# Overflow branch ahead of the experts, joint norm between two transformer blocks: one change to a float32 kernel on Trainium2

## What is computed

```python
def rms_norm(x, gain):                       # NORM_EPS = 1e-5
    xf = x.astype(jnp.float32)
    y = xf * lax.rsqrt(jnp.mean(xf * xf, axis=-1, keepdims=True) + NORM_EPS)
    return (y * gain.astype(jnp.float32)).astype(x.dtype)

# end of the first block
    for e in range(N_EXPERTS):
        out = out + combine[:, e:e + 1] * swiglu(t, w_gate[e], w_up[e], w_down[e])
    ...
    return rms_norm(h, final_norm)

# second block
    h = jnp.concatenate([meta, x], axis=1)
    for l in range(DEPTH):
        hn = rmsnorm(h, norm_gain[l])        # RMS_EPS = 1e-6
        proj = hn @ w_in[l]
    ...
        h = h + jnp.concatenate([do, fo], axis=-1) @ w_out[l]
    out = rmsnorm(h, final_gain)
    return out[:, N_META:N_META + seq]
```

## Time and profile before

| | us |
|---|---|
| median of 3 executions | 1854.92 |
| lowest, highest | 1848.85, 1860.95 |
| the profiled execution | 1859.74 |
| its span, first to last instruction | 1857.9 |
| TensorE busy | 1705.1 (92%) |
| VectorE busy | 1224.3 (66%) |
| ScalarE busy | 1029.4 (55%) |
| mean granted TensorE clock | 0.930 |

### The profile page before, as it was taken

The page is one execution under the profiler, slowest core; times in us unless marked ns, Lnnn a source line. Parts: engine busy times, 40 slices in busy tenths (PEclk is TensorE's granted clock), DMA queues, the critical chain, the costliest instruction groups (busy, mean ns, idle before and its releaser), DMA issues. The chain is left out here.

```text
span 1857.9 us, 21753 instructions
## 1 busy us (share of the span) xinstructions
PE 1705.1 (92%) x8749; PEld 1420.8 (76%) x8749; DVE 1224.3 (66%) x1305; ACT 1029.4 (55%) x1238; POOL 58.2 (3%) x54
## 2 busy tenths in 40 slices
PE   6988999887799999999999999999598999797997
PEld 5867888787678888888888888888397786587775
DVE  3645554468468888888888888888544544444553
ACT  4735443346367777777767677777544433444352
POOL 0000000013000000000000000000011000020000
PEclk9998999997789999999999999999799977798968
DMA  6323555550259999999999999999754222164200
GB/s 232 136 91 113 181 181 181 181 196 1 96 202 362 364 340 324 333 394 319 349 312 396 321 356 335 356 362 348 207 116 100 84 66 46 46 137 114 68 1 34
DMA packets 133081, 389.31 MB, mean 210 GB/s; under 512 B 8694, under 2 KB 14266, under 8 KB 132844
## 3 DMA queue, kind: packets, MB, share of 16 engines
q1 hardware_dynamic: 132692, 387.14, 61.7%
q10 hardware_dynamic: 280, 0.69, 0.1%
HBM read 386.76 MB, written 1.05 MB: 209 GB/s over the span
## 5 line engine op out<-in xcount | busy, mean ns | idle before, releaser
L192 DVE TENSOR_TENSOR wlo<-raw,whi 128x2048 fp32r<-128x2048 f32 (+1 forms) x286 | 629.1, 2208 | 304.4 <-ACT whi L182 303.0
L182 ACT ACTIVATE whi<-raw 128x2048 fp32r<-128x2048 f32 (+1 forms) x286 | 526.4, 1846 | 267.9 <-PE psum L359 267.9
L357 PE MATMUL psum<-whi,xh 128*128 128x512 f32 (+1 forms) x1280 | 499.8, 390 | 14.9 <-issue 8.6
L359 PE MATMUL psum<-whi,xl 128*128 128x512 f32 (+1 forms) x1280 | 488.6, 382 | 0.0
L358 PE MATMUL psum<-wlo,xh 128*128 128x512 f32 (+1 forms) x1280 | 488.1, 381 | 0.0
L357 PEld LDWEIGHTS psum<-whi,xh 128*128 128x128 f32 x1280 | 244.3, 191 | 72.1 <-DVE wlo L192 11.2
L359 PEld LDWEIGHTS psum<-whi,xl 128*128 128x128 f32 x1280 | 243.9, 191 | 50.3
L358 PEld LDWEIGHTS psum<-wlo,xh 128*128 128x128 f32 x1280 | 244.4, 191 | 46.7 <-issue 0.2
L192 DVE TENSOR_TENSOR wlo<-raw_more,whi 128x2048 fp32r<-128x2048 f32 (+1 forms) x94 | 204.0, 2177 | 39.5 <-ACT whi L182 38.7
L182 ACT ACTIVATE whi<-raw_more 128x2048 fp32r<-128x2048 f32 (+1 forms) x94 | 171.3, 1827 | 53.2 <-PE psum L359 53.2
L357 PE MATMUL psum<-xh,whi 128*128 128x256 f32 (+2 forms) x552 | 173.2, 314 | 11.5 <-DVE wlo L192 4.8
(11 more groups left out here) (334 smaller groups left out, 1579.5 us busy)
## 6 DMA issues: line engine op xcount, KB each, us to landing
raw<-in_moe_w_down_dram SPq DMA_DIRECT2D x58, 1024.0 KB, 7.6
raw<-in_moe_w_gate_dram SPq DMA_DIRECT2D x43, 1024.0 KB, 6.7
raw<-in_moe_w_up_dram SPq DMA_DIRECT2D x41, 1024.0 KB, 6.2
raw_more<-in_moe_w_down_dram SPq DMA_DIRECT2D x30, 1024.0 KB, 7.8
raw<-in_w_in_dram SPq DMA_DIRECT2D x28, 1024.0 KB, 7.6
raw_more<-in_moe_w_up_dram SPq DMA_DIRECT2D x23, 1024.0 KB, 6.4
raw_more<-in_moe_w_gate_dram SPq DMA_DIRECT2D x21, 1024.0 KB, 6.5
raw<-in_moe_w_up_dram SPq DMA_DIRECT2D x23, 768.0 KB, 5.9
```

The source lines that it names most:

```text
L182: act.e.activation(self.whi[:, i % self.ns, 0:kt * n], self.place[self.slots[i]][:, 0:kt * n], ACT.Copy, scale=1.0).then_inc(self.s_hi)
L192: dve.e.tensor_tensor(self.wlo[:, i % self.ns, 0:kt * n], self.place[self.slots[i]][:, 0:kt * n], self.whi[:, i % self.ns, 0:kt * n].bitca ...
L357: pe.e.matmul(o, lh, rh, start=start, stop=False)
L359: return pe.e.matmul(o, ll, rh, start=False, stop=stop)
```

## The change

1. `where_over` stands ahead of the experts on ScalarE, VectorE, TensorE and SyncE (on GpSimd too, whose work was already done), and waits for `flag` alone. The second pass gets a landing buffer of its own, and shares semaphores with stages that have ended.
2. In the routing the counts' matmuls come first, the flag is made earlier among VectorE's instructions, and the first `Pm` is made there (helper `places`) instead of at the start of the experts.
3. The transfers of the meta tokens and forget_bias go to the routing's list on SyncE, that of final_norm to a place among the last expert pieces, into a free half of a `raw_more` slot.
4. Between the blocks: with u = h · final_norm, the two norms become one factor: with a = mean(h²) + 1e-5, x · rsqrt(mean(x²) + 1e-6) = u / sqrt(mean(u²) + 1e-6 · a). VectorE makes u, ScalarE squares h and u in pieces of 128x512, one root serves both (four columns), and the first block's result H = u / sqrt(a) is written by ScalarE after the split of the turned tokens (`block1_out`).
5. The meta tokens' square, the table load of the square root and their root stand on ScalarE directly behind its last expert instruction.

The diff, cut to its core:

```diff
@@ make_route: order of the five matmuls, and VectorE @@
             pe.wait_ge(r.at("chosen"), (ld_c3, 32), xf_at(7))
+            pe.e.matmul(psum[:, 4, 0:8], ones, tp[:, 4, 0, :], start=True, stop=False)
+            pe.e.matmul(psum[:, 4, 0:8], ones, tp[:, 4, 1, :], start=False, stop=True).then_inc(s_pos)
             pe.e.matmul(psum[:, 3, 0:8], strict, tp[:, 4, 0, :], start=True, stop=True)
             pe.e.matmul(psum[:, 3, 8:16], ones, tp[:, 4, 0, :], start=True, stop=False)
-            pe.e.matmul(psum[:, 3, 8:16], strict, tp[:, 4, 1, :], start=False, stop=True)
-            pe.e.matmul(psum[:, 3, 16:24], ones, tp[:, 4, 0, :], start=True, stop=False)
-            pe.e.matmul(psum[:, 3, 16:24], ones, tp[:, 4, 1, :], start=False, stop=True).then_inc(s_pos)
+            pe.e.matmul(psum[:, 3, 8:16], strict, tp[:, 4, 1, :], start=False, stop=True).then_inc(s_pos)
...
+            dve.wait_ge(r.at("slot"), (ld_c3, 32))
+            places(dve, Pm0, 0, 0, 2).then_inc(moe_marks[0].end(0))
@@ make_route: sp @@
+            sp.e.dma_start(M, I["meta_tokens_2"]).then_inc(ld_m, 16)
+            for b in range(2):
+                sp.e.dma_start(fb[:, b:b + 1], I["forget_bias_2"][b].rearrange("(h o) -> h o", o=1)).then_inc(ld_fb, 16)
@@ where_over @@
-        p.wait_ge(*experts.ends, *route.ends, (s_flag, 1))
+        p.wait_ge((s_flag, 1))
         reg = p.e.alloc_register()
         p.e.reg_load(reg, flag[0:1, 0:1])
         with p.e.If_ne(reg, 0):
             inside = Program(p.e)
             inside.met = dict(p.met)
+            inside.wait_ge(*route.ends)
@@ the middle @@
     def mid_act(act):
-        squares(act, "fin", 0, [(H[:, j, :], 128) for j in range(2)], ox[:, 0:2, :].rearrange("p a b -> p (a b)"))
-        root(act, "fin", st[:, 0:2])
+        act.wait_ge(W.lo(fn_after), (ld_m, 16))
+        squares(act, "meta0", 2, [(M, 16)], raw_more[:, fn_slot - RAW, D:2 * D])
+        root(act, "meta0", st[0:16, 2:3])
+        for n, (t, c) in enumerate(((H, 40), (U, 48))):
+            for i, (j, half) in enumerate(HALVES):
+                act.wait_ge(*([u_dve.at(j, half), (m_sq, i + 1)] if n else [h_moe.at(NE - 1, j, half), experts.ends[0]]))
+                c_, o = c + half * 2 + j, (4 + i) % 6 * 512
+                act.e.activation(vvf[:, o:o + 512], part(t, j, half), ACT.Square, bias=0.0, scale=1.0,
+                                 accum_out=st[:, c_:c_ + 1]).then_inc(m_sq)
+        root(act, "b0", st[:, 52:56])
+        for half in range(2):
+            act.wait_ge(n_dve.at("b0", "rstd"))
+            act.e.activation(part(xn0, 1, half), part(U, 1, half), ACT.Identity, bias=0.0,
+                             scale=st[:, 53:54]).then_inc(s_xsa.end("b0", half))
...
+    def block1_out(act):
+        for j in range(2):
+            act.e.activation(H[:, j, :], U[:, j, :], ACT.Identity, bias=0.0, scale=st[:, 54 + j:55 + j]).then_inc(s_fin)
     def mid_dve(dve):
-        mean(dve, "fin", st[:, 0:2], D, 1e-5)
-        invert(dve, "fin", st[:, 0:2])
-        for j in range(2):
-            dve.wait_ge(n_dve.at("fin", "rstd"), (ld_fn, 16))
-            dve.e.scalar_tensor_tensor(H[:, j, :], H[:, j, :], st[:, j:j + 1], fn, ALU.mult, ALU.mult).then_inc(s_fin)
+        mean(dve, "meta0", st[0:16, 2:3], D, 1e-6)
+        invert(dve, "meta0", st[0:16, 2:3])
+        for j, half in HALVES:
+            dve.wait_ge(h_moe.at(NE - 1, j, half), experts.ends[0], (ld_fn, 16))
+            dve.e.tensor_tensor(part(U, j, half), part(H, j, half), part(fn.unsqueeze(1), 0, half),
+                                ALU.mult).then_inc(u_dve.end(j, half))
...
+        dve.e.scalar_tensor_tensor(st[:, 52:54], st[:, 0:2], 1.0 / D, st[:, 56:58], ALU.mult, ALU.add).then_inc(n_dve.end("b0", "mean"))
+        invert(dve, "b0", st[:, 52:56])
@@ the lists: SyncE; ScalarE, VectorE and TensorE alike @@
         route.sp(sp)
+        where_over(sp, over_sp)
+        W.follow(sp, fn_after + 1)
+        sp.wait_ge(W.lo(fn_after))
+        sp.e.dma_start(fn, I["final_norm"].partition_broadcast(128)).then_inc(ld_fn, 16)
         W.follow(sp, moe1 - 1 + NS)
-        where_over(sp, over_sp)
         mid_sp(sp)
...
-        for stage in (gla, dense, swa, route, experts):
+        for stage in (gla, dense, swa, route):
             stage.act(act)
         where_over(act, over.act)
+        experts.act(act)
         mid_act(act)
```

More of the change, by code:

```diff
@@ L115, in end, with count_on @@
         return self.sem
[L118 to L128, removed]
+def count_on(steps, names):
+    return Steps(steps.sem, names, max(steps.n.values()))
 class Weights:
@@ L1262, in make_route @@
         r = steps("route", ("logits",), *[(1, x) for x in best], ("rest",), *[(2, x) for x in best], ("chosen",),
-                  ("slots",), ("count",), ("slot",), ("diff",), ("sum",), ("inverse",), ("second",), ("w1",), ("w2",), ("cw",))
+                  ("diff",), ("sum",), ("inverse",), ("second",), ("count",), ("w1",), ("w2",), ("slots",), ("cw",), ("slot",))
         def xf_at(k):
@@ L1380, in make_route @@
-        return Stage(pe, act, dve, pool, sp, ends)
+            dve.wait_ge(r.at("slots"))
+            dve.e.tensor_scalar(sl2, sl2, -1.0, None, ALU.add).then_inc(r.end("slot"))
+            dve.wait_ge(r.at("slot"), (ld_c3, 32))
+            places(dve, Pm0, 0, 0, 2).then_inc(moe_marks[0].end(0))
+        ends = [(s_pos, 2), (s_exp, 1), r.at("slot"), (n_lo, 2)]
+        return Stage(pe, act, dve, pool, sp, ends)
+    M = cst[0:16, 256:256 + D]
+    fn_slot = min(range(RAW, RAW + MORE), key=lambda s: max(i for i, x in enumerate(slots) if x == s))
@@ L1382, in body, with places, make_experts @@
+    def places(dve, Pm, base, g, G):
+        for j in range(2):
+            for q in range(G):
+                ins = dve.e.tensor_scalar(Pm[:, j, q * 128:(q + 1) * 128], iota[:, :], float(base),
+                                          slot[:, j, g * G + q:g * G + q + 1], ALU.add, ALU.is_equal)
+        return ins
+    Pm0 = sb("Pm", [128, 2, 256], F32R, scope=moe)
+    moe_marks = [steps(f"moe_{name}", *names) for name, names in marks_of(2)]
     with ExitStack() as pre:
         route = make_route(pre)
-    def make_experts(tag, base, S, first, G, room):
+    def make_experts(base, S, first, G, room, marks, Pm):
@@ L1395, in make_experts @@
         yh = sb("yh", [128, D], F32R, scope=room)
+        with ExitStack() as same:
+            hid = sb("hid", [128, 1024], scope=same)
         yl = sb("yl", [128, D], F32R, scope=room)
@@ L1666, in body @@
         whi2, wlo2 = (sb(n, [128, 1, PW], F32R, scope=room) for n in ("whi2", "wlo2"))
-        W2nd = Weights(sem, "over", again, [0] * len(again), 1, whi2, wlo2, {0: raw_more[:, 0, :]})
-        over = make_experts("over", 128, W2nd, 0, G_OF["over"], room)
+        raw2 = sb("raw2", [128, PW], scope=room)
+        W2nd = Weights(sem, "over", again, [0] * len(again), 1, whi2, wlo2, {0: raw2})
+        over = make_experts(128, W2nd, 0, 1, room, [count_on(old, names) for old, (_, names) in zip(ended, marks_of(1))],
+                            Pm0[:, :, 0:128])
+    with ExitStack() as room:
+        experts = make_experts(0, W, moe0, 2, room, moe_marks, Pm0)
+        h_moe = moe_marks[-1]
     moe.close()
@@ L1735, in body @@
     b_out, dv_out = steps("dqk", *eights), steps("dv", *[(l, j) for l in range(2) for j in range(3)])
-    r_rot, r_sin, r_cos, r_add, r_hi, r_lo = (steps(f"rope_{x}", *eights) for x in ("turned", "sin", "cos", "added", "high", "low"))
+    r_rot, r_sin, r_cos, r_add, r_hi, r_lo = (count_on(old, eights) for old in ended_swa[0:6])
     g_out = steps("gates", *[(l, j) for l in range(2) for j in (4, 5, 6, 7, 0, 1, 2, 3, "silu")])
@@ L1918, in pe @@
                 pe.wait_ge(*layers[0].ends)
-            turn(pe, b, [(ox[0:16, 2, :], 16, 0), (ox[:, 0, :], 128, 16), (ox[:, 1, :], 128, 144)],
+            else:
+                pe.wait_ge(*experts.ends)
+            xn = xn0 if l == 0 else ox
+            turn(pe, b, [(ox[0:16, 2, :], 16, 0), (xn[:, 0, :], 128, 16), (xn[:, 1, :], 128, 144)],
                  scaled_at(b, s_meta.at(l)), {i: [] for i in range(8)})
@@ L2497, in _ @@
         Start.dve(dve)
-        for stage in (gla, dense, swa, route, experts):
+        for stage in (gla, dense, swa, route):
             stage.dve(dve)
-        where_over(dve, over.dve)
+        where_over(dve, over_dve)
+        experts.dve(dve)
         mid_dve(dve)
@@ L2519, in _ @@
         Start.pe(pe)
-        for stage in (gla, dense, swa, route, experts):
+        for stage in (gla, dense, swa, route):
             stage.pe(pe)
-        where_over(pe, over.pe)
+        where_over(pe, over_pe)
+        experts.pe(pe)
         for layer in layers:
```

143 lines of the change are left out of this document (80 added, 63 removed).

## The result

| | before | after |
|---|---|---|
| median, us | 1854.33 (10 executions) | 1843.50 (10 executions) |
| lowest, highest | 1846.33, 1860.95 | 1837.22, 1846.99 |
| profiled execution (its span) | 1859.74 (1857.9) | 1839.42 (1837.6) |

The ratio is 0.9941, with a 95% interval of 0.9922 to 0.9959: 7.6 to 14.5 us faster, 10.9 in the middle. The forecast was 1848, 7.1 less than the 1854.92 of the first three executions of before.

The account below looks back on a forecast made before the run. TensorE, busy 1705.1 of 1857.9 us, was taken as the bound, with gains only at the ends of the experts' stage. Joint -11.4 and routing +4.3 gave -7.1 us, from 1854.92 to 1847.8, named 1848; range 1838 to 1858.

Parts of the forecast that it names:

- The joint: From the experts' last addition to H to TensorE's turn of the tokens: branch and old norm chain removed, 11.4 us less.
- Early flag and `Pm`: Routing: flag ready 1.2 us earlier, `Pm` at 507.05; without a branch the gather would start 1.5 us earlier.
- The table load: Routing: ScalarE's table load falls between first gather and first `xh`, adding 1.3 us.
- The branch: Routing: priced at 6.65 us from the flag, so the gather starts at 511.65 instead of 508.67, 3.0 us later.
- The reason I gave for it: Jump distance doesn't decide the branch's price: SyncE over 58 rows and ScalarE over some 280 resume within 0.02 us.
- The sum: Whole kernel: -11.4 at the joint and +4.3 in the routing give -7.1 us.
- The cheap rival: Routing: branch hides behind slots and `Pm` and costs 0; sum -11.6, 1843 us; chance 0.20.
- The tail: From the turn of the tokens to the end, 515.5 us before: taken as unchanged.
- The work behind is the same, and so are its pauses: Argument against losing the gain behind the joint, where the granted clock is 0.85 on average.
- a change of this stretch by more than 3 us: Sign that the prediction is wrong: turn to end, 515.5 us before, changes by more than 3 us.
- the gain is lost in the phases behind: Rival, from 1353 us on: moved clock changes give 7 us back, 1855 us; chance 0.14.

Follow-up runs that it names:

- e2: After without any branch, all calls of `where_over` taken out, so no second pass for tokens past 128; 1840.98 us, ratio 0.9927.
- e1: After with the branch moved back to its old place behind the experts, all else kept; 1845.48 us, ratio 0.9949.
- e9: The kernel before, unchanged, profiled a second time; 1853.90 us.
- e3: After with one 8x1 activation directly behind ScalarE's branch, so the table load stands there; 1839.88 us, ratio 0.9914.
- e10: e1 with SyncE's remaining weight fetches and small tables held back until the first square behind the branch; 1856.03 us, ratio 1.0008.
- e7: After with a second register load, compare and jump over one wait, on ScalarE alone, ahead of the squares of H; 1848.02 us, ratio 0.9958.
- e4: After with 33 unused matmuls on TensorE ahead of its wait for the last combination; 1838.79 us, ratio 0.9908.
- e8: After with an unused register load on ScalarE, no jump, and SyncE's remaining fetches held back until the first square of H; 1850.50 us, ratio 0.9980.
- e5: After with e3's early table load, e4's fillers and filling matmuls in the routing (8, 18 and 12); 1835.17 us, ratio 0.9899.
- e12: e5 without the 12 fillers behind the counts and with 28 at the joint instead of 33; 1833.01 us, ratio 0.9904.

## Why the prediction was right, and which term was mis-sized

- **The joint.** Forecast -11.4 us, measured -11.5 (18.65 to 7.19, the same to 0.02 us in two profiles each). The parts hold as well, with small errors that cancel: root 0.08 us behind the last addition (0.3 to the first square was forecast, 0.19 measured), eight squares at 0.61 instead of 0.63, u hidden (its end at 1326.55 is 1326.6 on the scale of before, where 1328.4 was the limit), meta tokens' steps hidden; from the last sum to the turn 1.98 us (1328.86 to 1330.84) instead of 1.78. The lambda, c2 and final_norm transfers were costed at nothing, and no wait shows there for them.
- **Early flag and `Pm`.** Forecast -1.5 at the gather, measured -1.47 (3.84 against 5.31, e2 and e1). Further behind, at the last addition, it doesn't show (e9 above).
- **The table load.** Forecast +1.3, measured +1.28 in the chain; e3 takes it out.
- **The branch: the mis-sized term.** I took "its one measured price is 6.65 us" into the routing. It is 4.19 there: the gather moved by +0.35 us instead of +3.0. The step that failed is the choice between the ends: I noted that DMA was 100% busy at the one place and idle at the other, and took the value of the busy one all the same. In e10 the same jump at the old place costs 4.20 us once no transfer runs beside it, so the transfers are the difference.
- **The reason I gave for it** failed too. I wrote that the trace "doesn't agree that the distance decides", from SyncE jumping over 58 rows and ScalarE over some 280 and resuming together. Both were long jumps, I think, since a row of an ordered list can stand for many instructions; how many SyncE jumps over wasn't counted. Over a single wait ScalarE needs 0.73 us (e7), against 4.20 and 6.49 for the long jump (e10, e1). The rule of the Trainium skill ("Runtime: NRT & Kernel Launch", Instruction fetch mechanics), that a taken branch to a target outside what an engine holds forces a DMA fetch, agrees with these three numbers, and with packets of instructions at the long jumps (e1, e10) and none at the short one (e7).
- **The sum.** With 4.19 in place of 6.65 my own steps put the gather at 505.0 + 4.2 = 509.2, 0.5 later than before, and the sum at -11.4 + 0.5 + 1.3 = -9.6; by the rows of after it is -11.5 + 0.35 + 1.28 = -9.9. Measured: -10.8, interval -7.6 to -14.5. The forecast's -7.1 lies just outside it. The cheap rival's 1843 is nearer to the measured 1843.5 than my 1848, but by luck: in its mechanism the branch hides behind slots and `Pm` and costs nothing, and it costs 1.82 us beyond them. The truth lies between the two, and the tail adds what neither had.
- **The tail.** "The work behind is the same, and so are its pauses" held for the work, not for the clock. The windows from the turn to the end, before again (e9) and then after:

```profile
1336.70:1852.10 515.40, 456.40 (x2618) 382.85 (x2618) 246.23 (x488) 205.73 (x469) 27.83 (x32) 0.85 0.31 73
```

```profile
1330.80:1837.60 506.80, 446.43 (x2618) 374.45 (x2618) 246.02 (x488) 208.50 (x473) 27.73 (x32) 0.86 0.32 77
```

The same 2618 matmuls took 456.4 and 446.4 us of TensorE. Length times granted clock is nearly the same: summed over 126 equal windows of the tail it is 436.9 and 437.0 in the two profiles of before, 437.8 twice in after, and 436.3 (e1) to 438.7 (e4) in the others. So a tail that is shorter has less time at the low level and nothing else to it: 157 us in both profiles of before, 138 and 145 in after. Only where the transfers were held back the product is larger, 440.7 (e8 and e10).

I had named a change of this stretch by more than 3 us as a sign that the prediction is wrong, and it came: 515.5 to 506.8 and 510.2. The path of the sum that failed with it is "the work behind is the same, and so are its pauses", from which the tail was put at nothing. Little of the difference lies next to the joint: by the windows of 4 us the clock comes back at about 1347 in e9 (0.62 in 1344 to 1348), 10 us behind its turn, and at about 1339.6 in after (0.55 in 1336 to 1340), 9 us behind. The rest is scattered. That it belongs to the change isn't shown: e3 has the same joint as after and a tail of 516.0, as long as that of before, and the median of e3 is below that of after. The rival "the gain is lost in the phases behind" named the right place and, for the profiled executions, the wrong sign.

Open: whether e7 is really slower than after by more than the 0.73 us in its chain (its median is 4.5 us higher, the intervals of the ratios overlap, its tail of 516.1 is as long as e3's); where the two heaps of e1 get their different clock; how much of the 7 us in the tail of the profiled pairs is the change's; whether the long jump is as dear when one engine alone makes it.

## What to carry to other kernels

A price measured at one place holds only with what stood beside it: before moving a branch, look at the DMA queue at both places, since a long jump costs 4.2 us here with an idle queue and 6.5 beside weight transfers, and a short one 0.73 beside such transfers. Put such a branch where the engines wait for something else anyway, and give ScalarE a small operation behind it, so that a table load which the compiler puts after the branch falls into that wait. When a pause on TensorE can't be removed, a few matmuls without use in it, short enough to end before the wait does, keep the clock up (1.00 instead of 0.67 in e4). That they shorten the whole isn't shown here beyond what the early table alone gives: 0.9914 with it (e3), 0.9899 and 0.9904 with fillers too (e5, e12), against 0.9941 for after.

## What the runs showed of the hardware that I had not expected

- The price of this branch is nearly all in the long jump: load, compare and a jump over one wait took 0.73 us beside weight transfers (e7), the long one beside them 6.49 (e1) and 4.20 without (e10). Packets of instructions came late behind weight packets: none in 3.9 us while 744 of those passed (e1).
- Holding transfers back to clear the queue (e8, e10) shortened the jump by 2.3 us in e10 (4.20 against e1's 6.49), and the tail grew from 514.4 (e1) to 519.5 us.
- The tail, the same 2618 matmuls in every kernel, took from 503.3 us (e12) to 516.1 (e7) with no transfer held back, by its time at the low clock alone. That is more than most edits here move, so the stretches of a profile say what an edit does, and only the ratio over many executions what it is worth; with 6 to 11 executions each, the ratios here don't tell after from e1, e2, e3, e4 or e7.
